# Two-layer hybrid attention encoder on one core: in the differential-attention steps, the next step's scores move ahead of the filler projection

## The chip, the core and the metric

The kernel runs on one core of a Trainium2 chip. The metric is device time of one execution in microseconds, as the median of several runs. A core has TensorE (PE: matmuls, with its weight loads shown as PEld), VectorE (DVE), ScalarE (ACT), GpSimd (POOL) and SyncE (SP, here only the queue of the weight transfers). Each engine works through its own list of instructions in the order in which the kernel wrote them, and a semaphore wait at the head of one list holds everything behind it in that list.

## What is computed

An encoder of two layers on 512 tokens of width 1024. Each layer: RMSNorm; one input projection; latent attention with 8 heads and differential attention with 4 heads; output projection with residual; RMSNorm; squared-ReLU MLP with residual. The part that the change touches is the differential attention, per head `hd` and block of 128 query rows:

```
dq, dk: (512, 4 heads, 2 maps, 64);  dv: (512, 4 heads, 128)
bias = -slope[hd] * |qpos - kpos|
s    = einsum('bqhmd,bkhmd->bmhqk', qb, k) * 64**-0.5 + bias     # two maps m per head
p    = softmax(s, axis=-1)
w    = p[:, 0] - lam * p[:, 1]
o    = einsum('bhqk,bkhd->bqhd', w, v);  o = rmsnorm(o) * g_sub * (1 - lam_init)
...
latent:  q = c_q @ w_uq (+rope),  [k, v] = c_kv @ w_ukv          # rank 256, 8 heads
```

All matmuls are done in split precision: each operand is a high and a low float32r part, and a product is three matmuls (high·high, high·low, low·high; helper `three`, line 1509).

## The kernel before

Everything stays in SBUF; weights stream in as blocks of 512 KB through two stage buffers, ScalarE makes the high part of a block (`split`, L748), VectorE or GpSimd the low part (L1064). The projections of the later work are cut into pieces and used as **filler** on TensorE between the pieces of attention.

The attention of a layer is one list of 48 steps, written out by hand for each engine: steps 0 to 15 are the differential attention (4 heads by 4 query blocks), steps 16 to 47 the latent attention. The table `FILL` (L68 to L96) says which filler belongs to a step: steps 0 to 7 carry half a head projection each (dk2, dk2, dq2, dq2, dk3, dk3, dq3, dq3; 12 matmuls of 128x512), steps 8 to 14 one latent product each (v0, v1, kp0, q0, v2, v3, q1; 6 matmuls of 128x512).

I name the pieces of step n on TensorE: **F**n the filler; **S**n+1 the score pair of the next step (`score_pair`, L1548: six matmuls on 64 rows, the two maps beside each other); **T**n-1 the four transposes of the weights w of the step before (`turn`, L1577); in every fourth step **V** the values of a head (`values`, 12 matmuls, L1509 with pt and dv; V0, V1, V2 in steps 6, 10, 14), and in other steps the sums (`stat_c`, L1523, steps 8 and 12) and the spread of the norm (`stat_b`, L1534, steps 9 and 13). Before the change a step is F, S, sum or spread or V, T.

A score pair has to wait for `sc_free`: there are three score banks for two maps, so S n+1 cannot start before VectorE has read the first map of pair n. That reading is `ttr` (L1094: adds the bias, takes the row maximum, writes e to SBUF). After it ScalarE does the exponential (L759), VectorE the coefficients (`coef`, L1105, L1106), GpSimd scales and subtracts (L625, L628, the result is w), TensorE transposes w (T), ScalarE and VectorE split it into pt_hi and pt_lo (L780, L1124), and four of those make V.

VectorE's list in step n is: coef n-1, `ttr` of both maps of pair n, pt_lo of n-3, the low part of the filler that ended two steps ago together with the low part of a weight block (L1064), then the filler that ended one step ago (L1134, L1138, or for v and kp L1163, L1170), then in steps 8 and 12 `rc` (L1363, waits for stat_c), in steps 9 and 13 the norm's product (L1369, waits for stat_b). In steps 6, 10 and 14 pt_lo stands first, ahead of coef. A filler needs its own bank (`bank0_free` or `bank1_free`, in turn) and its weight block; F10 (kp0) takes the bank of F8 (v0), which VectorE frees with L1163.

Of the kernel before, what the change touches and what calls it, by code (L numbers as in the profile page):

```python
# [50 lines left out]
DSTEPS = DIFF_HEADS * TT  # L51
# [163 lines left out]
def trunk(nc, x, w_in, g_mix, g_q, g_kv, w_uq, w_ukv, lam_q1, lam_k1, lam_q2, lam_k2,  # L215
# [89 lines left out]
    with ExitStack() as ctx:  # L305
# [68 lines left out]
        def val(sem, l, k):  # L374

            return (l + 1) * per_layer[id(sem)] + k
# [75 lines left out]
        def d_keys(g):  # L452

            if g == DIFF_HEADS - 1:
                return dk_last[:, 0, :], dk_last[:, 1, :]
            return dk_hi[:, g, :], dk_lo[:, g, :]
# [1047 lines left out]
        def _(pe):  # L1504
# [14 lines left out]
            def stat_c(l, m, src=None):  # L1519

                pe.wait_ge(misc_free, val(misc_free, l, m))
                for tt in range(TT):
                    mm = nc.tensor.matmul(MISC_BANK[:, tt:tt + 1], (ss[:, tt * P:(tt + 1) * P] if src is None  # L1523
                                                                   else src[:, tt * P:(tt + 1) * P]),
                                          ones[:, 0:1], start=True, stop=True)
                mm.then_inc(misc_done, 1)

            def stat_b(l, m, k):

                pe.wait_ge(pow_done, val(pow_done, l, k + 1))  # L1530
                pe.wait_ge(misc_free, val(misc_free, l, m))
                src = rs if k else rs_mix
                for tt in range(TT):
                    mm = nc.tensor.transpose(MISC_BANK[:, tt * P:(tt + 1) * P], src[:, tt:tt + 1].to_broadcast([P, P]), ident[:, :])  # L1534
                mm.then_inc(misc_done, 1)

            def score_pair(l, n):

                hd, qt = divmod(n, TT)
                if qt == 0:  # L1540
                    pe.wait_ge(d_lo_made, val(d_lo_made, l, 2 * hd + 2))
                pe.wait_ge(sc_free, val(sc_free, l, 2 * n - 1))
                q = slice(qt * P, (qt + 1) * P)
                k_hi, k_lo = d_keys(hd)
                for p, (a, b) in enumerate(((dq_hi, k_hi), (dq_hi, k_lo), (dq_lo, k_hi))):
                    for m in range(2):
                        rows = slice(m * DIFF_D, (m + 1) * DIFF_D)
                        mm = nc.tensor.matmul(SC_BANKS[(2 * n + m) % 3][:, :], a[rows, hd, q], b[rows, :],  # L1548
                                              start=p == 0, stop=p == 2)
                        if p == 2:  # L1550
                            mm.then_inc(sc_done, 1)

            def scores(l, n):

                hd, qt = divmod(n - DSTEPS, TT)
                e = DSTEPS + n
                if qt == 0:
                    pe.wait_ge(q_lo_made, val(q_lo_made, l, hd + 1))
                    pe.wait_ge(krb_lo_made, val(krb_lo_made, l, 1))
                    if hd:  # L1560
                        pe.wait_ge(krb_copied, val(krb_copied, l, 16 if hd < 2 else 48))
                    pe.wait_ge(*read_out(l, f"kp{hd // 2}"))
                pe.wait_ge(sc_free, val(sc_free, l, e - 2))
                three(SC_BANKS[e % 3][:, :],
                      [(tuple(q[:, qt * P:(qt + 1) * P] for q in q_tile(hd)),
                        (k_pack[:, hd % 4, 0, :], k_pack[:, hd % 4, 1, :]))], True, True).then_inc(sc_done, 1)
# [46 lines left out]
            def head_sum(l, use, part):  # L1613

                high, low = block_ready(l, BLOCK_AT[(use, 0)])
                pe.wait_ge(*high)
                pe.wait_ge(*low)
                pe.wait_ge(*taken(l, use))
                for t in part:
                    mm = three(bank[BANK[use]][:, :], [(wtile(SLOT[BLOCK_AT[(use, 0)]], t), u(t))], t == 0, t == KD - 1)  # L1620
                if part[-1] == KD - 1:
                    mm.then_inc(proj_done, 1)

            def out_sum(l, use, part):

                j, name = int(use[4:]), use[:4]
                high, low = block_ready(l, BLOCK_AT[(name, j // 2)])
                pe.wait_ge(*high)
                pe.wait_ge(*low)
                pe.wait_ge(*taken(l, use))  # L1630
                s = SLOT[BLOCK_AT[(name, j // 2)]]
                for t in part:
                    n = t if name == "outd" else DIFF_HEADS + t
                    pe.wait_ge(o_lo_made, val(o_lo_made, l, n + 1))
                    w = tuple(x[:, s, t * 256 + (j % 2) * P:t * 256 + (j % 2 + 1) * P] for x in (w_hi, w_lo))
                    mm = three(bank[BANK[use]][:, :], [(w, o_tile(n))], t == 0, t == TT - 1)
                if part[-1] == TT - 1:
                    mm.then_inc(proj_done, 1)

            def latent_sum(l, use):  # L1640

                pe.wait_ge(*taken(l, use))
                acc = bank[BANK[use]][:, :]
                i = int(use.lstrip("vqkp"))
                terms = []
                for k in range(KC):
                    block_at = BLOCK_AT[("uq" if use[0] == "q" else "ukv", k)]
                    s = SLOT[block_at]
                    high, low = block_ready(l, block_at)
                    pe.wait_ge(*high)  # L1650
                    pe.wait_ge(*low)
                    if use[0] == "q":
                        terms.append((wtile(s, i), (c_hi[:, k, :], c_lo[:, k, :])))
                        continue
                    wv = [t[:, s, :] for t in (w_hi, w_lo)]
                    if use[0] == "k":
                        terms.append((tuple(w[:, i * P:(i + 1) * P] for w in wv), (c_hi[:, KC + k, :], c_lo[:, KC + k, :])))
                    else:
                        terms.append((tuple(c[:, KC + k, i * P:(i + 1) * P] for c in (c_hi, c_lo)),
                                      tuple(w[:, MLA_HEADS * NOPE:] for w in wv)))  # L1660
                three(acc, terms, True, True).then_inc(proj_done, 1)
# [53 lines left out]
            for l in layers(pe):  # L1715
# [64 lines left out]
                for n in range(STEPS + 1):  # L1780
                    if DSTEPS < n + 2 < STEPS:
                        scores(l, n + 2)
                    g, r = divmod(n - TT - 2, TT)
                    for use, part in FILL.get(n, []):
                        if use[0] == "d":
                            head_sum(l, use, part)
                        elif use[0] == "o":
                            out_sum(l, use, part)
                        else:
                            if use == "v0":  # L1790
                                pe.wait_ge(c_lo_made, val(c_lo_made, l, 2 * KC))
                            latent_sum(l, use)
                    if n >= STEPS - 1:
                        out_sum(l, OUTM_USES[n - STEPS + 1], range(0, 2))
                    if n + 1 < DSTEPS:
                        score_pair(l, n + 1)
                    if r == 2 and 0 <= g < DIFF_HEADS:
                        stat_c(l, MISC_AT[f"sub{g}_c"], tmp_s[:, 1, :])
                    if r == 3 and 0 <= g < DIFF_HEADS:
                        stat_b(l, MISC_AT[f"sub{g}_b"], 3 + g)  # L1800
                    if r == 3 and g >= DIFF_HEADS:
                        half_values(l, g + 1, 0)
                    if r == 0 and g == DIFF_HEADS:
                        half_values(l, g, 0)
                    if r == 0 and g >= 0:
                        values(l, g)
                    if n:
                        turn(l, n - 1)
                    if n + 2 == DSTEPS:
                        scores(l, n + 2)  # L1810
# [190 lines left out]
```

## Time and profile before

| | |
|---|---|
| time before, median of 3 runs | 1214.62 us (1214.17 to 1215.73) |
| the profiled execution itself | 1214.01 us, of which the span from first to last instruction 1211.7 us |
| TensorE busy | 1190.8 us, 98% of the span |
| VectorE, ScalarE, GpSimd busy | 875.1, 600.8, 581.4 us |
| mean granted TensorE clock | 0.997 of full speed |
| differential attention, first layer | about 80 to 158 us of the span |
| differential attention, second layer | about 676 to 755 us of the span |

A profile row of the timeline gives the start of an instruction from the start of the span, its duration, the engine, the line of kernel.py, what it writes and reads, and in brackets the idle time of the engine before it with the instruction that ended it. Matmuls overlap in the record, so on TensorE the distance between two starts says what a piece costs, not the duration. The same holds for short operations on VectorE, which follow each other about 0.6 us apart where their own durations read 0.69.

### The profile page before, as it was taken

How to read it: one execution, taken by the hardware profiler on the slowest of the kernel's cores; microseconds unless marked ns; L12 is line 12 of the kernel's file. 1: busy time of each engine (PE TensorE's matmuls, PEld its weight loads, DVE VectorE, ACT ScalarE, POOL GpSimd, SP SyncE). 2: the span in 40 equal slices, each digit the busy share in tenths (PEclk: the TensorE clock that was granted, in tenths of full speed). 3: DMA queues.
4: the chain of work that ended last, by engine and by line, in shares of the span. 5: the costliest groups of instructions: out<-in, count | busy, mean ns of one | idle time of the engine just before them, and what ended most of it. 6: DMA issues, size and time to landing. Idle time of an engine off the chain costs nothing.

```text
span 1211.7 us, 16408 instructions
## 1 busy us (share of the span) xinstructions
PE 1190.8 (98%) x5700; PEld 974.7 (80%) x5700; DVE 875.1 (72%) x1349; ACT 600.8 (50%) x986; POOL 581.4 (48%) x371
## 2 busy tenths in 40 slices
PE   8999999999999999999999999999999999999997
PEld 7877678888888888888888766788888888888886
DVE  4657867656778776879846677776657778767896
ACT  6346666744544344435423466677444444344443
POOL 1004554622865576556510245536047665766462
PEclk9999999999999999999999999999999999999999
DMA  6421110124224322430324201102252234223402
GB/s 187 130 68 61 45 27 26 54 87 157 73 87 136 118 87 84 130 108 32 104 59 120 70 27 44 36 18 88 78 166 88 86 105 139 88 75 117 140 10 95
DMA packets 128131, 104.55 MB, mean 86 GB/s; under 512 B 5514, under 2 KB 107956, under 8 KB 128052
## 3 DMA queue, kind: packets, MB, share of 16 engines
q1 hardware_dynamic: 127840, 103.50, 28.5%
q8 instruction: 47, 0.77, 0.3%
q14 instruction: 32, 0.26, 0.1%
q10 hardware_dynamic: 84, 0.02, 0.0%
q0 software_dynamic: 128, 0.00, 0.0%
HBM read 99.84 MB, written 2.10 MB: 84 GB/s over the span
## 4 chain that ended last, share of the span: by engine, by line
PE 93%; DVE 3%; POOL 1%; issue 1%; ACT 1%; DMA 1%; SPq 0%; POOLq 0%; ACTq 0%; DVEq 0%
PE bank L1509 83%; PE bank L1577 3%; PE bank L1605 3%; PE bank L1548 2%; PE bank L1523 1%; DVE pt_lo L1124 1%; PE bank L1740 1%; DMA xin<-in_x 1%; PE bank L1534 0%; ACT pt_hi L780 0%; DVE k_pack L1170 0%; PE bank L1685 0%; POOL rs L619 0%; DVE dq_lo L1177 0%; POOL e_x L628 0%
## 5 line engine op out<-in xcount | busy, mean ns | idle before, releaser
L1509 PE MATMUL bank<-u_hi,w_hi 128*128 128x512 f32 x760 | 299.4, 394 | 0.3
L1509 PE MATMUL bank<-u_hi,w_lo 128*128 128x512 f32 x760 | 296.0, 390 | 0.0
L1509 PE MATMUL bank<-u_lo,w_hi 128*128 128x512 f32 x760 | 295.8, 389 | 0.0
L748 ACT ACTIVATE w_hi<-stage 128x1024 fp32r<-128x1024 f32 (+2 forms) x141 | 136.4, 976 | 221.1 <-DMA stage<-in_w_up 91.6
L1064 DVE TENSOR_TENSOR w_lo<-stage,w_hi 128x1024 fp32r<-128x1024 f32 (+2 forms) x116 | 137.4, 1193 | 60.4 <-ACT w_hi L748 60.0
L1509 PEld LDWEIGHTS bank<-u_hi,w_hi 128*128 128x128 f32 x760 | 142.7, 188 | 30.8 <-issue 2.5
L1509 PEld LDWEIGHTS bank<-u_hi,w_lo 128*128 128x128 f32 x760 | 142.6, 188 | 30.1
L1509 PEld LDWEIGHTS bank<-u_lo,w_hi 128*128 128x128 f32 x760 | 142.8, 188 | 28.6
L748 ACT ACTIVATE w_hi<-b 128x1024 fp32r<-128x1024 f32 x84 | 88.9, 1059 | 131.7 <-PE bank L1509 107.8
L1509 PE MATMUL bank<-w_hi,quad_hi 128*128 128x512 f32 x392 | 152.6, 389 | 0.0
L1509 PE MATMUL bank<-w_hi,quad_lo 128*128 128x512 f32 x392 | 152.5, 389 | 0.0
L1509 PE MATMUL bank<-w_lo,quad_hi 128*128 128x512 f32 x392 | 152.5, 389 | 0.0
L1064 DVE TENSOR_TENSOR w_lo<-b,w_hi 128x1024 fp32r<-128x1024 f32 x84 | 121.7, 1449 | 24.5 <-ACT w_hi L748 24.5
L1454 DVE TENSOR_TENSOR acc<-acc,bank 128x512 f32<-128x512 f32 x216 | 136.9, 680 | 0.0
L1124 DVE TENSOR_TENSOR pt_lo<-bank,pt_hi 128x512 fp32r<-128x512 f32 x96 | 66.1, 688 | 49.1 <-ACT pt_hi L780 48.7
L1468 DVE SCALAR_TENSOR_TENSOR tmp_y<-bank,rb 128x512 f32<-128x512 f32 x64 | 43.7, 689 | 69.2 <-PE bank L1509 68.5
L619 POOL TENSOR_TENSOR rs<-rc,mhalf 128x4 f32<-128x4 f32 x14 | 17.0, 1215 | 157.2 <-DVE rc L1079 143.2
L1509 PEld LDWEIGHTS bank<-w_lo,quad_hi 128*128 128x128 f32 x392 | 73.6, 188 | 15.4
L1509 PEld LDWEIGHTS bank<-w_hi,quad_lo 128*128 128x128 f32 x392 | 73.6, 188 | 15.2
L1509 PEld LDWEIGHTS bank<-w_hi,quad_hi 128*128 128x128 f32 x392 | 73.6, 188 | 15.2
L646 POOL TENSOR_TENSOR b<-b,b 128x1024 f32<-128x1024 f32 x28 | 81.6, 2913 | 2.0 <-DMA b<-in_w_down 1.0
L634 POOL TENSOR_SCALAR e_t<-e_t,coefs 128x512 f32<-128x512 f32 x64 | 44.2, 692 | 69.6 <-DVE coefs L1118 68.7
(236 smaller groups left out, 2287.0 us busy)
## 6 DMA issues: line engine op xcount, KB each, us to landing
stage<-in_w_up SPq DMA_DIRECT2D x64, 512.0 KB, 4.0
b<-in_w_down SPq DMA_DIRECT2D x56, 512.0 KB, 3.4
stage<-in_w_in SPq DMA_DIRECT2D x32, 512.0 KB, 3.9
stage<-in_w_out SPq DMA_DIRECT2D x16, 512.0 KB, 3.5
stage<-in_w_down SPq DMA_DIRECT2D x8, 512.0 KB, 3.4
xin<-in_x SPq DMA_DIRECT2D x4, 512.0 KB, 6.7
stage<-in_w_ukv SPq DMA_DIRECT2D x4, 512.0 KB, 3.8
out<-yout SPq DMA_DIRECT2D x8, 256.0 KB, 2.3
```

The lines of the kernel that those rows point to most:

```text
L619: nc.gpsimd.tensor_tensor(dst[:, :], rc[:, :], mhalf[:, :], ALU.pow).then_inc(pow_done, 1)
L634: nc.gpsimd.tensor_scalar(e_t[:, t, :], e_t[:, t, :], coefs[:, t:t + 1], 1.0, ALU.mult, ALU.mult).then_inc(p_ready, 1)
L646: nc.gpsimd.tensor_tensor(dst[:, :], a[:, :], b[:, :], ALU.subtract).then_inc(t_made, 1)
L748: last = nc.scalar.activation(hi(w_hi, s)[:, :, d:d + n], st(r)[:, :, f:f + n], ACT.Copy)
L1064: last = nc.vector.tensor_tensor(dst, st(r)[:, :, f:f + n], hi(w_hi, s)[:, :, d:d + n].bitcast(F32), ALU.subtract)
L1124: nc.vector.tensor_tensor(piece(pt_lo), TR_BANKS[n % 2].rearrange("p (k c) -> p k c", k=TT), piece(pt_hi).bitcast(F32), ALU.subtract).then ...
L1454: last = nc.vector.tensor_tensor(dst, dst, src, ALU.add)
L1468: nc.vector.scalar_tensor_tensor(out=tmp_y[:, i % 2, :], in0=bank[BANK[use]][:, :], scalar=0.0, in1=rb[:, :], op0=ALU.max, op1=ALU.mult).t ...
L1509: mm = nc.tensor.matmul(acc, a, b, start=first and t == 0 and m == 0, stop=last and t == len(terms) - 1 and m == 2)
L1548: mm = nc.tensor.matmul(SC_BANKS[(2 * n + m) % 3][:, :], a[rows, hd, q], b[rows, :], start=p == 0, stop=p == 2)
L1577: mm = nc.tensor.transpose(TR_BANKS[n % 2][:, kt * P:(kt + 1) * P], e_slot(t)[:, kt * P:(kt + 1) * P], ident[:, :])
L1605: mm = nc.tensor.matmul(MISC_BANK[:, q], v_pack[:, kt, hd, :, :].rearrange("p a c -> p (a c)"), pt[:, kt, q], start=(kt == 0 and pt is pt_ ...
```

## The change

In the step loop of TensorE the call of `score_pair(l, n + 1)` moves from behind the filler to ahead of it. Nothing else is edited: the number of instructions of every engine, their shapes, all semaphores and the orders of VectorE, ScalarE, GpSimd and SyncE are the same. It applies to the 15 steps 0 to 14 of each of the two layers, since a later step has no score pair.

```
@@ -1781,6 +1781,8 @@
                     if DSTEPS < n + 2 < STEPS:
                         scores(l, n + 2)
                     g, r = divmod(n - TT - 2, TT)
+                    if n + 1 < DSTEPS:
+                        score_pair(l, n + 1)
                     for use, part in FILL.get(n, []):
...
                         out_sum(l, OUTM_USES[n - STEPS + 1], range(0, 2))
-                    if n + 1 < DSTEPS:
-                        score_pair(l, n + 1)
```

TensorE, first layer, step 10, before: the last rows of T8, then F10 (reads c and w), S11 (reads dk and dq), and the first matmul of V1 (reads pt and dv). The semaphores that a matmul waits for stand in brackets.

```order
L1577 MATMUL bank<-ident,e_x 128x128 x3
L1509 MATMUL bank<-c_hi,w_hi 128x512 [waits w_hi_made,w_lo_dve,bank1_free]
L1509 MATMUL bank<-c_lo,w_hi 128x512
L1509 MATMUL bank<-c_hi,w_lo 128x512
...
L1548 MATMUL bank<-dk_hi,dq_hi 128x512 [waits sc_free]
L1548 MATMUL bank<-dk_hi,dq_hi 128x512
L1548 MATMUL bank<-dk_lo,dq_hi 128x512 x2
L1548 MATMUL bank<-dk_hi,dq_lo 128x512 x2
L1509 MATMUL bank<-pt_hi,dv_hi 128x512 [waits misc_free,pt_lo_made]
```

The same place with the change:

```order
L1577 MATMUL bank<-ident,e_x 128x128 x3
L1548 MATMUL bank<-dk_hi,dq_hi 128x512 [waits sc_free]
L1548 MATMUL bank<-dk_hi,dq_hi 128x512
L1548 MATMUL bank<-dk_lo,dq_hi 128x512 x2
L1548 MATMUL bank<-dk_hi,dq_lo 128x512 x2
L1509 MATMUL bank<-c_hi,w_hi 128x512 [waits w_hi_made,w_lo_dve,bank1_free]
L1509 MATMUL bank<-c_lo,w_hi 128x512
L1509 MATMUL bank<-c_hi,w_lo 128x512
...
L1509 MATMUL bank<-pt_hi,dv_hi 128x512 [waits misc_free,pt_lo_made]
```

The wait for `sc_free` now stands directly behind T8, and the six matmuls of the filler stand behind it, next to the values.

TensorE, first layer, step 9, before: the last rows of T7, then F9, S10, and the spread (`stat_b`).

```order
L1577 MATMUL bank<-ident,e_t 128x128 x3
L1509 MATMUL bank<-w_hi,c_hi 128x512 [waits w_hi_made,w_lo_dve,bank0_free]
L1509 MATMUL bank<-w_lo,c_hi 128x512
L1509 MATMUL bank<-w_hi,c_lo 128x512
...
L1548 MATMUL bank<-dk_hi,dq_hi 128x512 [waits sc_free]
L1548 MATMUL bank<-dk_hi,dq_hi 128x512
L1548 MATMUL bank<-dk_lo,dq_hi 128x512 x2
L1548 MATMUL bank<-dk_hi,dq_lo 128x512 x2
L1534 MATMUL bank<-ident,rs 128x128 [waits misc_free,pow_done]
```

The same place with the change:

```order
L1577 MATMUL bank<-ident,e_t 128x128 x3
L1548 MATMUL bank<-dk_hi,dq_hi 128x512 [waits sc_free]
L1548 MATMUL bank<-dk_hi,dq_hi 128x512
L1548 MATMUL bank<-dk_lo,dq_hi 128x512 x2
L1548 MATMUL bank<-dk_hi,dq_lo 128x512 x2
L1509 MATMUL bank<-w_hi,c_hi 128x512 [waits w_hi_made,w_lo_dve,bank0_free]
L1509 MATMUL bank<-w_lo,c_hi 128x512
L1509 MATMUL bank<-w_hi,c_lo 128x512
...
L1534 MATMUL bank<-ident,rs 128x128 [waits misc_free,pow_done]
```

Here too the filler has moved from ahead of the wait for `sc_free` to behind the score pair; the sum of the step before, T7 and the spread keep their places in the list.

## Rows read from the trace of the kernel before

**Rows 1.** Page, the chain that ended last: shares of the span by engine.

```profile
PE 93%; DVE 3%; POOL 1%; issue 1%; ACT 1%; DMA 1%; SPq 0%; POOLq 0%; ACTq 0%; DVEq 0%
```

**Rows 2.** Timeline, TensorE, step 4 (start, us, engine, line, what, count, idle before).

```profile
102.90 0.47 PE L1509 MATMUL bank<-u_hi,w_hi 128*128 128x512 f32 x1
...
105.84 0.50 PE L1548 MATMUL bank<-dk_hi,dq_hi 64*128 64x512 f32 x2
...
106.74 0.66 PE L1577 MATMUL bank<-ident,e_t 128*128 128x128 f32 x4
107.15 0.47 PE L1509 MATMUL bank<-u_hi,w_hi 128*128 128x512 f32 x1
```

**Rows 3.** Timeline, TensorE, steps 8 to 11 of the first layer.

```profile
124.21 0.50 PE L1548 MATMUL bank<-dk_hi,dq_hi 64*128 64x512 f32 x2
...
126.01 0.63 PE L1577 MATMUL bank<-ident,e_t 128*128 128x128 f32 x4
...
127.96 0.50 PE L1548 MATMUL bank<-dk_hi,dq_hi 64*128 64x512 f32 x2
...
130.20 0.66 PE L1577 MATMUL bank<-ident,e_x 128*128 128x128 f32 x4 [0.69 <-POOL e_x L628]
132.02 0.50 PE L1509 MATMUL bank<-c_hi,w_hi 128*128 128x512 f32 x1 [1.17 <-DVE v_pack L1163]
...
134.06 0.50 PE L1548 MATMUL bank<-dk_hi,dq_hi 64*128 64x512 f32 x2 [0.38 <-DVE nmx L1094]
...
137.82 0.60 PE L1577 MATMUL bank<-ident,e_t 128*128 128x128 f32 x4
```

**Rows 4.** Timeline, VectorE, steps 7 to 14 of the first layer.

```profile
120.16 1.35 DVE L1064 TENSOR_TENSOR w_lo<-stage,w_hi 128x768 fp32r<-128x768 f32 x3
...
126.53 0.67 DVE L1094 CUSTOM_DVE_ANT_0 e_t<-bank,consts 128x512 f32<-128x512 f32 x1
...
128.94 2.43 DVE L1064 TENSOR_TENSOR w_lo<-stage,w_hi 128x768 fp32r<-128x768 f32 x3
...
133.33 0.67 DVE L1094 CUSTOM_DVE_ANT_0 e_t<-bank,consts 128x512 f32<-128x512 f32 x1
...
141.60 0.69 DVE L1094 CUSTOM_DVE_ANT_0 e_t<-bank,consts 128x512 f32<-128x512 f32 x1
...
145.26 0.67 DVE L1094 CUSTOM_DVE_ANT_0 e_t<-bank,consts 128x512 f32<-128x512 f32 x1
...
148.79 0.74 DVE L1369 SCALAR_TENSOR_TENSOR tmp_s<-tmp_s,gsl,bank 128x512 f32<-128x512 f32 x1
...
150.24 0.67 DVE L1094 CUSTOM_DVE_ANT_0 e_x<-bank,consts 128x512 f32<-128x512 f32 x1
```

**Rows 5.** Timeline, GpSimd, the same stretch.

```profile
128.37 1.77 POOL L628 TENSOR_TENSOR e_x<-e_x 128x512 f32<-128x512 f32 x1
```

**Rows 6.** Timeline, TensorE, steps 12 to 16 of the first layer.

```profile
144.74 0.63 PE L1577 MATMUL bank<-ident,e_x 128*128 128x128 f32 x4
...
150.98 0.73 PE L1548 MATMUL bank<-dk_last,dq_hi 64*128 64x512 f32 x4 [0.19 <-DVE nmx L1094]
...
154.73 0.60 PE L1577 MATMUL bank<-ident,e_t 128*128 128x128 f32 x4
...
158.14 1.05 PE L1523 MATMUL bank<-ones,tmp_s 128*128 128x1 f32 x8 [0.29 <-ACT tmp_s L821]
```

**Rows 7.** Windows: stretch, length, busy of PE, PEld, DVE, ACT, POOL, then granted clock.

```profile
724.90:728.80 3.90, 2.05 (x13) 1.48 (x12) 3.90 (x7) 1.12 (x4) 1.27 (x1) 0.99 0.11 14
728.80:732.20 3.40, 3.40 (x11) 1.80 (x11) 2.93 (x11) 2.04 (x5) 2.25 (x3) 0.50 0.86 285
130.20:132.00 1.80, 0.65 (x4) 0.41 (x4) 1.80 (x5) 0.00 (x0) 0.00 (x0) 1.00 0.00 0
```

**Rows 8.** Timeline, TensorE, steps 10 and 11 of the second layer.

```profile
728.04 0.50 PE L1509 MATMUL bank<-c_hi,w_hi 128*128 128x512 f32 x1 [1.17 <-DVE v_pack L1163]
...
734.89 0.60 PE L1577 MATMUL bank<-ident,e_t 128*128 128x128 f32 x4
```

More of the change, by code:

```diff
@@ L1783, in _ @@
                     g, r = divmod(n - TT - 2, TT)
+                    if n + 1 < DSTEPS:
+                        score_pair(l, n + 1)
                     for use, part in FILL.get(n, []):
@@ L1794, in _ @@
                         out_sum(l, OUTM_USES[n - STEPS + 1], range(0, 2))
-                    if n + 1 < DSTEPS:
-                        score_pair(l, n + 1)
                     if r == 2 and 0 <= g < DIFF_HEADS:
```

## The prediction

> **What bounds the kernel now.** I read three views. The chain that ended last says that TensorE holds 93% of the span [rows 1]: whatever keeps TensorE idle counts in full. Then TensorE's timeline through the differential attention of the first layer. In steps 1 to 8 it never waits: step 4 costs 2.94 us for F, 0.90 for S and 0.41 for T [rows 2], and the other steps with twelve-matmul fillers repeat this. From step 9 on the fillers are only six matmuls and TensorE starts to wait: 0.69 us before T8 for w from GpSimd, 1.17 us before F10 for the bank that VectorE's v_pack frees, 0.38 us before S11 for the score bank [rows 3]. The third view, VectorE's own list, says why: between the score readings at 126.53 and 133.33 it works without a gap, 2.43 us of it on one weight block [rows 4]. So steps 9 to 14 are bound by VectorE's list, and TensorE has just enough other work in between. The second layer repeats the pattern 596 us later.
>
> **The sequence, written as a ring.** Before, TensorE does T(n-2), F(n), S(n+1), T(n-1); with the change T(n-2), S(n+1), F(n), T(n-1). Nothing is added or removed, no DMA moves, and no other engine's list changes. Three things change: which kinds of matmul are neighbours; T(n-1) gets one filler more between its scores and itself; and S(n+1) loses the filler that stood right before its wait for `sc_free`. Between S(n) and S(n+1) there stood T and F(n), now F(n-1) and T: equally much work, but one filler earlier against VectorE's list wherever VectorE is late.
>
> **Term 1, the neighbours: a small gain.** A filler after transposes and before scores costs 2.94 us [rows 2]; the twelve matmuls of V1, which stand between scores and transposes, cost 137.82 - 134.06 - 0.90 = 2.86 [rows 2, 3]. So the moved filler saves 0.08. Transposes directly followed by 64-row scores are in no row. Bounds: the transposes cost the same 0.41, or up to 0.1 more; the whole effect per step then lies between -0.08 and +0.02, and I take -0.05 to -0.06, since both neighbours of S already pay their turn today. Over the nine steps up to the sum of step 8 that is 0.5 us per layer: that sum ends at 125.5 instead of 126.01 [rows 3]. Limits: 0.8 earlier to 0.2 later.
>
> **Term 2, S10: nothing.** From here I replay the first layer against VectorE's list. VectorE starts the reading of pair 9 0.52 us after the sum of step 8 ends (126.53 against 126.01) [rows 3, 4], now at 126.0. A score pair starts 0.73 us after the reading that it waits for has begun (S11 134.06 against 133.33) [rows 3, 4]. So S10 starts at 126.75, where its place is free at 125.9: a new wait of 0.8 us. It costs nothing, because T8 waits for GpSimd's w, which hangs on that same sum: T8 comes at 130.2 - 0.5 = 129.7 (its releaser began at 128.37 and took 1.77 [rows 5]). S10, F9 (126.01 to 127.96 less 0.4 for T7, so 1.5) and the spread (0.4, four transposes like T) end at 126.75 + 0.9 + 1.5 + 0.4 = 129.55. The wait before T8 shrinks by what S10 waits for.
>
> **Term 3, S11: the main loss.** T8 ends at 130.1. S11 needs the reading of pair 10, which VectorE reaches at 133.33 - 0.5 = 132.8, so S11 starts at 133.55: TensorE stands still for 3.4 us. Before, F10 ran in part of this hole (132.02 to 134.06 with S11's wait). Now it comes after S11: S11 to 134.45, F10 (1.5) to 135.95, V1 (2.75 behind another matmul) to 138.7. Before it ended at 137.82 [rows 3]. So step 10 loses 0.9 us, although the step began 0.5 us early: the filler's 1.4 us are uncovered.
>
> **Term 4, S13: more of it.** VectorE and ScalarE wait for V1 before they can overwrite pt, so the reading of pair 12 follows the end of V1 by 141.60 - 137.82 = 3.8 us [rows 3, 4], now at 142.5. T9 and S12 and F11 and T10 run from 138.7 to 141.9 (0.4, 0.9, 1.5, 0.4), S13 has to stand until 142.5 + 0.73 = 143.2. Then S13 to 144.1, F12 to 145.6, the sum (124.21 to 126.01 less 0.9, so 0.9 [rows 3]) to 146.45. T11 stood at 144.74 [rows 6]: 1.7 us late.
>
> **Term 5, S14 and S15.** The reading of pair 13 follows that sum by 0.52 (145.26 against 144.74 [rows 4, 6]): S14 starts at 147.7 instead of following T11 at 146.9. S14, F13 and the spread end at 150.5. VectorE's product with the spread (148.79 before) is followed 1.45 us later by the reading of pair 14 (150.24) [rows 4]; with 150.6 for the product, S15 starts at 150.6 + 1.45 + 0.73 = 152.8 instead of 150.98 [rows 6]. S15, F14 and V2 end at 152.8 + 0.9 + 1.5 + 2.75 = 157.9. Before it was 154.73 [rows 6]. **Loss per layer: 3.2 us**, rounded to 3.1 for small parts that I rounded up.
>
> **Term 6, is it given back?** The next wait of TensorE, before the sum at 158.14, is for ScalarE's square of what stands behind V2 [rows 6]. It moves with V2, so the loss stays. From step 16 on the order is as it was. Two layers: +6.2 us. Limits per layer: 1.9 and 4. The lower one: VectorE's weight block of step 9 took 2.43 us, the same three instructions one block earlier 1.35 [rows 4]; if it fell to 1.35, S11 would come 1.1 us earlier. The row shows that the long one began inside GpSimd's 1.77 us [rows 4, 5] and ended about 1.2 us after it. Both follow the sum of step 8, so I keep 2.43. The Trainium skill's page "SBUF — State Buffer", section "Who interferes with whom", says that a VectorE operation with two SBUF inputs and a GpSimd operation that reads SBUF exclude each other for a whole instruction; by that rule the block stays at 2.43 as long as GpSimd begins first, and the trace agrees with it.
>
> **Term 7, TensorE's clock.** In the second layer, after a stretch in which TensorE had 2.05 us of work in 3.90, the granted clock fell to 0.50 for 3.4 us (728.8 to 732.2); in the same place of the first layer it stayed at 1.00 [rows 7]. That is 1.2 instead of 2.4 GHz. Its cost is read from F10 to T9: 6.85 us there (728.04 to 734.89), 5.80 in the first layer [rows 3, 8], so 1.05. With a hole of 3.4 us in the same place, and work without a pause behind it, I expect the low clock in both layers. Half speed for 3.4 us of full work costs 1.7, the row shows 1.05; I take 1.4. The first layer pays 1.4, the second 1.4 - 1.05 = 0.35, since it pays already. Sum 1.75 us; limits -1.05 (high clock in both) and +2.4. "TensorE: Matmul & The Clock Gate" of the Trainium skill, in "Part 1: The HAM clock gate", says that idling throttles the array to half rate and sustained work releases it; by that page the longer hole makes the low clock more likely, and one row here agrees while another, with a shorter hole, shows no drop.
>
> **The sum.** 6.2 + 1.75 = 8.0 us. The span of 1211.7 becomes 1219.7, the profiled execution of 1214.01 becomes 1222.0, and the median, 0.6 above it, 1222.6.
>
> **Rivals.** (a) *The waits come, the clock doesn't fall further.* If neither layer falls: 6.2 - 1.05 = +5.1, 1219.8; if one does, near 1221. For it: the first layer's hole left the clock at 1.00 [rows 7]. Against: the new hole is twice as long. (b) *VectorE is earlier than in my replay*, as by the 1.35 us block: 3.1 - 1.1 = 2.0 per layer, +4.0 and little from the clock, 1218.6. Against: the lists of VectorE and GpSimd keep their order. (c) *No change that can be told.* The early scores let VectorE pull its readings forward everywhere, and S11 finds its bank free soon enough that F10 loses only what T8 and F10 wait for now: the 0.7 and 1.2 us [rows 3] pay for it, 1214.6. Against: between 126.53 and 133.33 VectorE has no gap to pull anything into [rows 4]. (d) *Faster.* T has one filler more before it. If the waits before T8 (0.69) and F10 (1.17) [rows 3] really went and nothing came in their place, each layer would win 1.9 less what the next step returns, about 1.2, with 0.5 of Term 1 on top: -3.4 us, 1211.2. It decides at one point: VectorE would have to start the reading of pair 10 by 129.4, so that S11 follows T8 at 130.1; it starts at 132.8. (e) *Worse*: the low clock comes a second time at the holes before S13 and S15, 1.4 in each layer, 1225.4.
>
> **How the numbers follow.** Forecast (both layers with the low clock) 45%; (a) 23%; (b) 12%; (c) 8%; (d) 6%; (e) 6%. The range leaves out (c) and (d) and the far end of (e): 1217.0 to 1225.5, which holds about 82%; its lower end is (b) with a limit of Term 1, its upper end the forecast with 1.7 per low clock, a loss of 4 in one layer, and (e). A measurement of this kernel can tell about 0.2%, 2.4 us: slower by more takes the forecast, (a), (e) and most of (b), 0.84; within 0.2% takes (c) and a little of (b), 0.10; faster 0.06.
>
> **What would show it.** In the changed profile: steps 1 to 8 of a layer at about 4.2 us without a wait; a wait before S10 of under 1 us; a wait of some 3.4 us before S11, released by VectorE's L1094, in place of the waits before F10; S13 and S15 with waits of 1 to 2 us; V2 of the first layer ending near 157.9; a granted clock of 0.5 behind S11 in both layers. I am wrong if S11 starts within 1 us of T8's end, if V2 ends before 155.5, or if the delay is gone again by step 20.

## The result and the profile after

| | before | changed |
|---|---|---|
| median | 1214.39 us, 4 runs (1213.85 to 1215.73) | 1229.01 us, 4 runs (1224.91 to 1229.34) |
| profiled execution | 1214.01 us | 1229.19 us |
| its span | 1211.7 us | 1226.8 us |
| mean granted clock | 0.997 | 0.991 |

The changed kernel is slower: ratio 1.0106, 95% interval 1.0094 to 1.0118, which is 12.9 us (11.4 to 14.3). The two medians are 14.6 us apart and the spans of the two profiled executions, which are taken apart below, 15.1 us. The forecast was slower by 8.0 us (1222.6), with a range up to 1225.5. The direction holds, the size doesn't.

The page of the changed kernel: the span, then the busy time of each engine. TensorE is busy for 98% of the span, the same share as before. But its busy time rose from 1190.8 to 1197.9 us with the same 5700 matmuls: at a low clock a matmul is busy for longer. This is the first hint that about half of the loss isn't waiting.

```profile
span 1226.8 us, 16408 instructions
...
PE 1197.9 (98%) x5700; PEld 982.8 (80%) x5700; DVE 877.9 (72%) x1349; ACT 602.0 (49%) x986; POOL 581.5 (47%) x371
```

**Steps 1 to 8.** Timeline of TensorE of the changed kernel, step 4 (columns as in [rows 2]). F, then T, then the scores directly behind T, then the next F:

```profile
103.54 0.50 PE L1509 MATMUL bank<-u_hi,w_hi 128*128 128x512 f32 x1
...
106.44 0.60 PE L1577 MATMUL bank<-ident,e_t 128*128 128x128 f32 x4
106.97 0.50 PE L1548 MATMUL bank<-dk_hi,dq_hi 64*128 64x512 f32 x2
...
107.86 0.50 PE L1509 MATMUL bank<-u_hi,w_hi 128*128 128x512 f32 x1
```

F took 106.44 - 103.54 = 2.90 where it was 2.94 [rows 2]. S took 0.89 as before. T took 106.97 - 106.44 = 0.53 where it was 0.41. The step grew from 4.25 to 4.32 us. No step up to 7 has a wait.

**Steps 8 to 15.** The same view, first layer, to be laid beside [rows 3] and [rows 6]. Scores are L1548, transposes L1577, the sum behind V2 L1523:

```profile
125.78 0.63 PE L1577 MATMUL bank<-ident,e_t 128*128 128x128 f32 x4
127.03 0.50 PE L1548 MATMUL bank<-dk_hi,dq_hi 64*128 64x512 f32 x2 [0.62 <-DVE nmx L1094]
...
129.99 0.66 PE L1577 MATMUL bank<-ident,e_x 128*128 128x128 f32 x4
133.85 0.80 PE L1548 MATMUL bank<-dk_hi,dq_hi 64*128 64x512 f32 x2 [3.21 <-DVE nmx L1094]
...
141.70 0.60 PE L1577 MATMUL bank<-ident,e_t 128*128 128x128 f32 x4
...
146.24 0.74 PE L1548 MATMUL bank<-dk_last,dq_hi 64*128 64x512 f32 x4 [0.99 <-DVE nmx L1094]
...
150.69 0.73 PE L1548 MATMUL bank<-dk_last,dq_hi 64*128 64x512 f32 x4 [0.61 <-DVE nmx L1094]
...
155.90 0.73 PE L1548 MATMUL bank<-dk_last,dq_hi 64*128 64x512 f32 x4 [1.79 <-DVE nmx L1094]
...
162.63 0.60 PE L1577 MATMUL bank<-ident,e_t 128*128 128x128 f32 x4
...
166.04 1.05 PE L1523 MATMUL bank<-ones,tmp_s 128*128 128x1 f32 x8 [0.28 <-ACT tmp_s L821]
```

The waits before T8 (0.69) and F10 (1.17) of [rows 3] are gone. In their place S10 waits 0.62, S11 3.21, S13 0.99, S14 0.61 and S15 1.79, each for VectorE's reading of an earlier score pair: 7.2 us in all.

VectorE's own timeline of the changed kernel shows that it is no earlier than before. These are the reading of pair 9, the weight block and the reading of pair 10, the ones of [rows 4]:

```profile
126.30 0.67 DVE L1094 CUSTOM_DVE_ANT_0 e_t<-bank,consts 128x512 f32<-128x512 f32 x1
...
128.70 2.45 DVE L1064 TENSOR_TENSOR w_lo<-stage,w_hi 128x768 fp32r<-128x768 f32 x3
...
133.12 0.67 DVE L1094 CUSTOM_DVE_ANT_0 e_t<-bank,consts 128x512 f32<-128x512 f32 x1
```

The reading of pair 10 moved from 133.33 to 133.12 and no further. VectorE's timeline shows no gap from 126.30 to there.

**The clock.** Windows of the changed kernel (columns as in [rows 7]; behind the clock come the share of DMA and its GB/s). The first three follow the hole before S11; then come the low stretch behind S15, the one behind S11 in the second layer, and one that comes later in that layer:

```profile
130.70:133.00 2.30, 0.00 (x0) 0.00 (x0) 2.30 (x7) 0.00 (x0) 0.00 (x0) 1.00 0.28 55
133.00:133.90 0.90, 0.05 (x2) 0.05 (x2) 0.90 (x6) 0.07 (x1) 0.59 (x1) 0.52 1.08 375
133.90:139.70 5.80, 5.80 (x16) 4.18 (x17) 2.60 (x9) 1.97 (x5) 3.50 (x4) 0.50 0.29 101
157.00:160.50 3.50, 3.50 (x9) 2.76 (x9) 1.55 (x7) 0.92 (x3) 2.54 (x3) 0.52 0.00 0
737.30:744.10 6.80, 5.73 (x16) 4.11 (x17) 3.72 (x14) 2.04 (x5) 4.10 (x4) 0.51 0.43 145
771.00:774.50 3.50, 3.50 (x13) 2.72 (x11) 0.78 (x2) 1.27 (x3) 2.53 (x3) 0.55 0.01 2
```

TensorE did nothing from 130.7 to 133.0. At about 133.0 the granted clock fell to 0.5, that is 1.2 instead of 2.4 GHz, while TensorE was still idle. It stayed there until 139.7, through 5.8 us of work without a pause. It came once more from 157.0 to 160.5. In the second layer it lasted again 6.8 us behind S11 and 3.5 us after the attention steps. This execution has 20.5 us of it. The kernel before had the 3.4 us of [rows 7] and as much again near the start of its profiled execution, where the changed kernel had none. The same window of both, before and then changed:

```profile
8.50:12.00 3.50, 3.50 (x14) 2.59 (x13) 2.58 (x5) 2.38 (x5) 0.00 (x0) 0.51 1.14 323
8.50:12.00 3.50, 3.50 (x20) 2.89 (x19) 3.04 (x5) 3.05 (x6) 0.00 (x0) 1.00 1.15 324
```

Both kernels have the same instructions in the same order there, so this isn't the change's doing. But the same matmuls, from the first of L1685 to the first of L1705, took 6.40 us before (10.07 to 16.47) and 5.55 in the changed kernel (10.29 to 15.84). This is why the changed kernel's first layer begins early: its first score pair stands at 79.38 instead of 80.02, and 0.63 of these 0.64 us are there at 16 us already.

**The price of the low clock** is read from pieces with the same instructions. S11 to T9 takes 141.70 - 133.85 = 7.85 us. In a run below whose clock stayed up (the one with idle matmuls) it takes 139.12 - 134.00 = 5.12: 2.73 us lost. S15 to T13 takes 162.63 - 155.90 = 6.73 against 158.54 - 153.43 = 5.11 in that run: 1.62 lost. The second layer:

```profile
738.37 0.79 PE L1548 MATMUL bank<-dk_hi,dq_hi 64*128 64x512 f32 x2 [3.21 <-DVE nmx L1094]
...
746.04 0.60 PE L1577 MATMUL bank<-ident,e_t 128*128 128x128 f32 x4
...
760.24 0.73 PE L1548 MATMUL bank<-dk_last,dq_hi 64*128 64x512 f32 x4 [1.79 <-DVE nmx L1094]
...
765.36 0.60 PE L1577 MATMUL bank<-ident,e_t 128*128 128x128 f32 x4
...
770.69 0.66 PE L1577 MATMUL bank<-ident,e_t 128*128 128x128 f32 x4 [0.86 <-POOL e_t L628]
```

Here S11 to T9 takes 7.67 (2.55 lost) and S15 to T13 5.12 (nothing lost). From the 770.69 on to the last values takes 6.18, in the kernel before 4.60: 1.58 lost. In all 8.5 us, where the kernel before loses 1.05 in the second layer and the 0.64 of its start.

### The profile page after: what moved, and what is told of

The parts are those of the page before. It is cut to its first block, busy times and chain, and to the rows that moved or that the text cites. A ratio compares the mean times of both kernels' runs of the same rounds, so it can differ in the third digit from the quotient of the medians.

```text
span 1226.8 us, 16408 instructions
## 1 busy us (share of the span) xinstructions
PE 1197.9 (98%) x5700; PEld 982.8 (80%) x5700; DVE 877.9 (72%) x1349; ACT 602.0 (49%) x986; POOL 581.5 (47%) x371
## 4 chain that ended last, share of the span: by engine, by line
PE 94%; DVE 3%; issue 1%; ACT 1%; POOL 1%; DMA 0%; POOLq 0%; SPq 0%; ACTq 0%; DVEq 0%
PE bank L1509 83%; PE bank L1577 3%; PE bank L1605 2%; PE bank L1548 2%; PE bank L1523 1%; DVE pt_lo L1124 1%; PE bank L1534 1%; PE bank L1740 1%; PE bank L1677 0%; DMA xin<-in_x 0%; ACT pt_hi L780 0%; DVE k_pack L1170 0%; PE bank L1685 0%; DVE dq_lo L1177 0%; PE bank L1893 0%
## 5 line engine op out<-in xcount | busy, mean ns | idle before, releaser
L1064 DVE TENSOR_TENSOR w_lo<-stage,w_hi 128x1024 fp32r<-128x1024 f32 (+2 forms) x116 | 137.0, 1190 | 60.6 <-ACT w_hi L748 60.1
L1454 DVE TENSOR_TENSOR acc<-acc,bank 128x512 f32<-128x512 f32 x216 | 137.0, 680 | 0.0
L780 ACT ACTIVATE pt_hi<-bank 128x512 fp32r<-128x512 f32 x96 | 57.1, 594 | 49.7 <-PE bank L1509 30.8
```

The source lines that it names most:

```text
L780: nc.scalar.activation(pt_hi[:, :, q * P:(q + 1) * P], TR_BANKS[n % 2].rearrange("p (k c) -> p k c", k=TT), ACT.Copy).then_inc(pt_hi_made, 1)
L1064: last = nc.vector.tensor_tensor(dst, st(r)[:, :, f:f + n], hi(w_hi, s)[:, :, d:d + n].bitcast(F32), ALU.subtract)
L1454: last = nc.vector.tensor_tensor(dst, dst, src, ALU.add)
```

## The experiments

Each ran in five rounds beside the kernel before. They were measured in three groups. The kernel before had medians of 1215.26, 1215.76 and 1215.90 us in these, and a ratio is always against the runs of the same group.

**Which steps carry the loss.** The move was made in some steps only. In all of these the edit has one form; the condition is all that differs:

```diff
-                    if n + 1 < DSTEPS:
+                    if n + 1 < DSTEPS and <condition>:
                         score_pair(l, n + 1)
                     for use, part in FILL.get(n, []):
...
+                    if n + 1 < DSTEPS and not (<condition>):
+                        score_pair(l, n + 1)
                     if r == 2 and 0 <= g < DIFF_HEADS:
```

Only the steps with long fillers, condition `n < 8`:

> The score pair is moved ahead of the filler only in steps 0 to 7 (twelve-matmul fillers), steps 8 to 14 stand as before. My theory: in these steps TensorE has no holes, so only the junction of transposes and scores costs, 0.06 us in each of some six steps per layer: 1214.4 + 0.8 = 1215.2 us, no wait in steps 1 to 8, clock as before. Rival (the whole delay comes from the long fillers now ending late against VectorE and ScalarE): most of the 14.6 us is here, 1222 us or more.

Measured 1215.71 us, ratio 1.0001 (0.9993 to 1.0010). The long fillers cost nothing that can be told. TensorE's timeline of this run still shows what the new neighbours cost: T8 stands at 130.20, as in [rows 3], although the layer's first score pair, which stands in the same place in every kernel, began at 79.58 instead of 80.02 us; 0.44 us went on the way. It also shows the low clock in a place where the kernel before had none in its profiled execution. This is S11 with 0.80 instead of 0.50 per pair of matmuls, and T9 at 138.88 instead of 137.82 [rows 3]:

```profile
130.20 0.66 PE L1577 MATMUL bank<-ident,e_x 128*128 128x128 f32 x4 [0.69 <-POOL e_x L628]
...
134.19 0.80 PE L1548 MATMUL bank<-dk_hi,dq_hi 64*128 64x512 f32 x2
...
138.88 0.60 PE L1577 MATMUL bank<-ident,e_t 128*128 128x128 f32 x4
```

So the order before brings the low clock from time to time too, and the 1.05 us of Term 7 are read here a second time.

Only the steps from 8 on, condition `n >= 8`:

> The score pair is moved only in steps 8 to 14. My theory: the holes before S11, S13 and S15 and the low clock behind them come back in full, 14.6 less 0.8 = +13.8, 1228.2 us. Rival (long fillers): under +4, 1218 us at most.

Measured 1228.2 us (1226.63 to 1229.74), ratio 1.0107 (1.0093 to 1.0121), the same as the whole change. The loss lies where TensorE waits for VectorE. The hole before S11 was 3.21 us here too. In the first layer of this execution S11 to T9 took 6.65 us, 1.5 more than at the full clock, where the changed kernel lost 2.7; in the second it took 7.92, 2.8 more.

Only step 10, condition `n == 10`:

> The score pair is moved in step 10 alone. My theory: S11 starts when VectorE has read pair 10, as before at about 134 us, and F10 comes behind it: V1 is 1.5 us later per layer, and the hole of about 3.4 us before S11 brings the low clock, 2.7 us in the first layer and 1.6 more in the second: 3.0 + 4.3 = +7.3, 1221.7 us; without the low clock +3, 1217.4. Rival (it is the sum of small shifts in all of steps 8 to 14, each of which takes from the next): about a seventh of the whole, +2, 1216.5 us.

Measured 1221.5 us, ratio 1.0051 (1.0037 to 1.0065), +6.2. TensorE's timeline of this run, the transposes of step 8 and the scores S11 behind them, then T9:

```profile
130.07 0.66 PE L1577 MATMUL bank<-ident,e_x 128*128 128x128 f32 x4 [0.69 <-POOL e_x L628]
133.94 0.80 PE L1548 MATMUL bank<-dk_hi,dq_hi 64*128 64x512 f32 x2 [3.21 <-DVE nmx L1094]
...
141.89 0.60 PE L1577 MATMUL bank<-ident,e_t 128*128 128x128 f32 x4
```

One moved score pair in each layer gives the full hole of 3.21 us. Up to T8 nothing differs from [rows 3], where it stands at 130.20 with the same wait of 0.69. T9 comes at 141.89 instead of 137.82: 1.4 us for the filler that no longer runs in the hole, and 2.8 for the clock (S11 to T9 takes 7.95 instead of 5.12), less the 0.1 by which S11 came earlier. The hole doesn't come from the steps ahead.

Only step 9, condition `n == 9`:

> The score pair is moved in step 9 alone. My prediction says that this is free: S10 waits 0.8 us, but T8 waits for GpSimd's w in any case, and nothing else is late: within 0.5 us of before, T8 at the same time. Rival (every early wait costs what it lasts): +0.8 per layer, +1.6 us.

Measured 1216.0 us, ratio 1.0002 (0.9994 to 1.0011). S10 waits for VectorE in this run too (0.61 us), and this costs nothing: T7 to T8 takes 4.21 us (127.86 to 132.07), before it took 4.19 [rows 3]. The wait of 0.69 before T8 is gone, so S10 now waits in the time in which T8 used to wait for GpSimd. F10's wait for v_pack is still 1.16, as in [rows 3].

Only steps 12 and 14, condition `n in (12, 14)`:

> The score pair is moved in steps 12 and 14 alone. My theory (the loss sits where a filler is taken from in front of a wait that VectorE ends): S13 starts 0.73 us after the reading of pair 12 begins (141.6), at 142.3, and F12 behind it ends 0.9 us later than S13 did; S15 starts at 151.0 as before, with F14 (1.4 us) behind it: 2.3 us per layer, 4.6 in all, and the hole of 1.8 us before S15 brings a low clock of 1.6 us in about one of the layers: 1215.3 + 4.6 + 1.6 = 1221.5 us, 1219.9 without it. Rival (step 10 is the one place, and the later waits only follow from it): no wait before S13 and S15 of over 0.5 us, 1216 us.

Measured 1221.7 us (1220.12 to 1221.9), ratio 1.0051 (1.0038 to 1.0063), +5.8. The scores S13 and S15 and the T13 behind V2:

```profile
142.16 0.73 PE L1548 MATMUL bank<-dk_last,dq_hi 64*128 64x512 f32 x4 [1.06 <-DVE nmx L1094]
...
151.60 0.74 PE L1548 MATMUL bank<-dk_last,dq_hi 64*128 64x512 f32 x4 [1.57 <-DVE nmx L1094]
...
156.73 0.60 PE L1577 MATMUL bank<-ident,e_t 128*128 128x128 f32 x4
```

S13 waits 1.06 and S15 1.57, though nothing was moved in step 10, and T13 comes 2.0 us later than the 154.73 of [rows 6] at a full clock. This layer began 0.27 us earlier (first score pair at 79.75), so it lost 2.3, as was expected. Of the 5.8 us some 4.5 are this, and the low clock, which this execution shows twice in the second layer, can account for the rest.

All steps but 10, 12 and 14, condition `n not in (10, 12, 14)`:

> The score pair is moved in all of the steps 0 to 14 but 10, 12 and 14. My theory: the waits that appear before S10 and S14 are covered by the waits for GpSimd before T8 and T12, and only the junction of transposes and scores is left, about 0.06 us in each of some nine steps per layer: 1215.3 + 1 = 1216.3 us. Rival (the move costs something wherever it stands): eleven fifteenths of the 14.6 us less the low clock, +5 or more, 1220 us.

Measured 1217.27 us, ratio 1.0007 (0.9998 to 1.0016), +1.4. That isn't clear of noise. Its runs fall into two sets: five from 1214.3 to 1215.8 us with a mean clock of 0.998, six from 1217.3 to 1218.0 with 0.995. The profiled one is of the second set and had the low clock from 8.1 to 15.0 us, ahead of everything that was moved. The three parts sum to 6.2 + 5.8 + 1.4 = 13.4 us, where the whole cost 14.6 in its own runs and 12.9 as steps 8 on. The rival that the loss is spread over all steps, and Term 1's gain, both fall; three steps carry some nine tenths of it.

**Is it the clock?** In the changed kernel the holes were filled with idle matmuls. Twelve stand ahead of S11, four ahead of S13, seven ahead of S15. They write into the first of the two banks that the scores are about to fill, once that is free:

```diff
-                pe.wait_ge(sc_free, val(sc_free, l, 2 * n - 1))
+                pe.wait_ge(sc_free, val(sc_free, l, 2 * n - 2))
...
+                for _ in range({11: 12, 13: 4, 15: 7}.get(n, 0)):
+                    nc.tensor.matmul(SC_BANKS[2 * n % 3][:, :], dq_hi[:, hd, q], k_hi, start=True, stop=True)
+                pe.wait_ge(sc_free, val(sc_free, l, 2 * n - 1))
```

> The changed kernel with idle-filling matmuls (128x512 on operands already in SBUF, into the bank that S writes next) in the holes: 12 before S11, 4 before S13, 7 before S15, each behind the wait for that bank and ahead of the wait for VectorE. They add 23 matmuls per layer and no result. My theory (the low clock is a cost of its own beside the waits): the granted clock stays at 1.00 and the kernel gains 2.7 + 1.6 in the first layer and 2.6 + 1.6 in the second, 8.5 together: 1220.5 us, V2 of the first layer ends 4 us earlier. Rival (the waits are the cost, the low clock only fills time that TensorE would wait in anyway): within 1 us of the changed kernel, 1229 us; it could also be slower, if the extra matmuls push the scores later.

Measured 1222.79 us (1221.94 to 1225.14), ratio 1.0064 (1.0052 to 1.0076): 6.2 us less than the changed kernel, with 46 matmuls more, whose products are not used. TensorE's timeline and the windows (scores are L1551 here, transposes L1580, the idle matmuls L1546):

```profile
130.55 3.01 PE L1546 MATMUL bank<-dk_hi,dq_hi 128*128 128x512 f32 x12
134.00 0.50 PE L1551 MATMUL bank<-dk_hi,dq_hi 64*128 64x512 f32 x2 [0.44 <-DVE nmx L1094]
...
139.12 0.60 PE L1580 MATMUL bank<-ident,e_t 128*128 128x128 f32 x4
...
153.43 0.74 PE L1551 MATMUL bank<-dk_last,dq_hi 64*128 64x512 f32 x4 [0.19 <-DVE nmx L1094]
...
158.54 0.60 PE L1580 MATMUL bank<-ident,e_t 128*128 128x128 f32 x4
```

```profile
130.50:134.00 3.50, 3.06 (x15) 2.20 (x13) 3.50 (x11) 0.02 (x1) 0.55 (x1) 1.00 0.41 126
134.00:140.00 6.00, 6.00 (x32) 4.60 (x34) 2.65 (x9) 2.65 (x7) 3.58 (x4) 1.00 0.29 102
764.00:767.40 3.40, 3.28 (x10) 2.77 (x11) 1.21 (x3) 1.58 (x4) 2.96 (x4) 0.54 0.01 2
```

S11 starts at 134.00, 0.15 later than in the changed kernel, still released by VectorE. T8 was 0.15 later already (130.14), so the idle matmuls put nothing on top: T8 to S11 takes 3.86 us in both. But T9 comes at 139.12 instead of 141.70 and T13 at 158.54 instead of 162.63. The clock stood at 1.00 through the hole and after it. One low stretch remained in this execution, after the differential attention of the second layer. The forecast of 8.5 us less had none in it. It costs 1.6 us, as in the changed kernel, and that is what separates this execution (1222.15) from the expected 1220.5; the median lies 0.6 above it. So the rest of the loss is there without the clock: this span of 1220.3 less 1.6 is 1218.7, and the span before, 1211.7 less its own 1.05 and 0.64, is 1210.0. That leaves 8.7 us, and some 7 of the 15.1 for the clock.

The same cure for the kernel before, five idle matmuls in the gap between T8 and F10:

```diff
+                    if n == 10:
+                        pe.wait_ge(sc_free, val(sc_free, l, 2 * n))
+                        for _ in range(5):
+                            nc.tensor.matmul(SC_BANKS[2 * (n + 1) % 3][:, :], dq_hi[:, n // TT, 0:P], d_keys(n // TT)[0], start=True, stop=True)
                     for use, part in FILL.get(n, []):
```

> The kernel before with five matmuls that give no result (128x512, into the bank of S11) between T8 and F10, where TensorE stands idle for 1.4 us. My theory (low clock as a cost of its own): the second layer's low clock at 728 to 732 us, 1.05 us, does not come: -1, 1213.9 us. Rival (the hole is not what brings it): no change, and 0.5 granted clock in the same place.

Measured 1215.65 us, ratio 0.9996 (0.9987 to 1.0005): a miss. The windows say why:

```profile
130.00:133.00 3.00, 2.99 (x13) 1.84 (x11) 3.00 (x9) 0.00 (x0) 0.14 (x1) 1.00 0.37 101
160.00:163.50 3.50, 3.50 (x10) 2.63 (x9) 0.47 (x1) 1.18 (x3) 2.24 (x3) 0.51 0.00 0
```

The place that was filled kept its clock, in both layers. But the low clock came elsewhere in that execution, at 160.0 and again at 757.3, each behind a wait of 0.86 us for GpSimd. Filling one gap of a chain with several doesn't buy the 1 us.

**Is it VectorE's list?** The weight block of step 9 stands on VectorE ahead of the reading of pair 10. It was moved behind the reading of pair 11, to the end of step 10. Its user comes much later. This was done on the kernel before and on the changed one:

```diff
-                    split(l, BLOCK_AT[(use, 0)] + RING)
+                    if use != HEAD_USES[-1]:
+                        split(l, BLOCK_AT[(use, 0)] + RING)
...
                         elif use[0] not in "vk":
                             gen(l, use)
+                    if n == 10:
+                        split(l, BLOCK_AT[(HEAD_USES[-1], 0)] + RING)
```

> The kernel before, with one edit on VectorE: the low part of the last query-weight block (L1064, 2.43 us in step 9) is made at the end of step 10 instead, behind the readings of pair 10 and v1. My theory (VectorE's list in steps 9 and 10 sets when TensorE goes on): v_pack frees F10's bank at about 129.5 instead of 131.9 and the reading of pair 10 begins at 131.0 instead of 133.3; F10 follows T8 at once, V1 ends at 135.4 instead of 137.8: 2.4 us per layer and the second layer's low clock (1) go: -5.8, 1209 us. Rival (the waits before F10 and S11 are only shown there, the chain through GpSimd and ScalarE sets the pace): within 1 us of before.

Measured **1209.11 us** (1207.95 to 1210.89), ratio 0.9946 (0.9934 to 0.9958), the fastest kernel of this case. TensorE's timeline, the starts of F10 (L1512 here), S11 and T9:

```profile
130.33 0.48 PE L1512 MATMUL bank<-c_hi,w_hi 128*128 128x512 f32 x1
...
131.90 0.50 PE L1551 MATMUL bank<-dk_hi,dq_hi 64*128 64x512 f32 x2
...
135.66 0.60 PE L1580 MATMUL bank<-ident,e_t 128*128 128x128 f32 x4
```

VectorE's, the reading of pair 10 and the moved block:

```profile
130.72 0.67 DVE L1094 CUSTOM_DVE_ANT_0 e_t<-bank,consts 128x512 f32<-128x512 f32 x1
...
132.53 1.74 DVE L1064 TENSOR_TENSOR w_lo<-stage,w_hi 128x768 fp32r<-128x768 f32 x3
```

The reading starts at 130.72 instead of 133.33 [rows 4]. F10 and S11 follow each other and T8 without a wait, and T9 comes at 135.66 instead of 137.82 [rows 3]. T8 (129.92) was 0.28 earlier already, so a layer gains 1.9 us and not the 2.4 that I expected. The rest goes with the clock: its mean was 0.999, and the profiled execution has no low stretch at all before its idle end.

> The changed kernel with the same edit. My theory: the reading of pair 10 begins at about 131.4, S11 starts at 132.1 instead of 133.9, the hole before it falls from 3.4 to 1.7 us and leaves the clock high: 1.7 us of waiting and 2.6 us of low clock less per layer: 1229 - 8.6 = 1220.4 us; it stays slower than the same edit on the kernel before, by about 11 us, since S13 and S15 still wait ahead of their fillers. Rival (the changed order is bad whatever VectorE does): gain as small as on the kernel before, 5 us at most, 1224 us.

Measured 1222.45 us (1218.6 to 1224.57), ratio 1.0052 (1.0039 to 1.0065), 6.6 less than the changed kernel but 2 more than expected. TensorE's timeline, S11 and T9:

```profile
132.43 0.50 PE L1551 MATMUL bank<-dk_hi,dq_hi 64*128 64x512 f32 x2 [1.59 <-DVE nmx L1094]
...
139.15 0.60 PE L1580 MATMUL bank<-ident,e_t 128*128 128x128 f32 x4
```

and a window of the same run:

```profile
132.00:137.00 5.00, 4.57 (x15) 3.41 (x16) 4.65 (x14) 2.05 (x5) 3.31 (x4) 0.66 0.10 17
```

The hole before S11 shrank from 3.2 to 1.6 us and T9 came 2.5 us earlier. But in this layer the clock fell all the same, for half as long (133.6 to 137.0); in the second, behind a hole of 1.6 us too, it stayed up. Two more low stretches came at 164.3 and at 754. Even with VectorE unloaded the changed order is 13 us behind the old one: S13 and S15 still wait 1.0 and 1.8 us.

## Why the prediction was right about the sign and short by half

**Term 1, the neighbours: wrong in sign.** I bounded the transposes in front of 64-row scores at up to 0.1 more and took a gain for the step. They cost 0.12 more (0.53 against 0.41), F gave back 0.04 and not 0.08, and the step grew by 0.07. From the layer's first score pair (79.38, before 80.02) to T8 (129.99, before 130.20) the changed kernel takes 0.43 us more, in the second layer 0.39, where 0.5 less was forecast. Two layers: 1.8 us of the miss.

**Term 2, S10: right.** Forecast: S10 at 126.75 with a wait of 0.8, free of charge, T8 at 129.7. Measured: 127.03, 0.62, 129.99. The run with step 9 alone shows the wait and no loss.

**Term 3, S11: right.** Forecast: a hole of 3.4 us, S11 at 133.55, by L1094. Measured: 3.21 and 133.85. The run with step 10 alone shows that this one move makes the hole. V1 was to end at 138.7; with the clock held up it ended at 139.12, with the low clock at 141.70.

**Terms 4 and 5, S13 to S15: right but for the clock.** S13, S14, S15 and the end of V2 were forecast at 143.2, 147.7, 152.8 and 157.9. Take the 2.73 us of clock behind S11 from the measured times, and for the end of V2 the 1.62 of the second low stretch too: 143.5, 148.0, 153.2 and 158.3. All are 0.3 to 0.4 late: the 0.9 of Term 1 less the 0.64 by which this execution's first layer began early. That they lie so close is in part luck, since those two cancel. The run with idle matmuls has the end of V2 at 158.54. The 3.1 us per layer stand but for the 0.9 of Term 1.

**Term 6, not given back: right.** T13 comes 7.9 us later than in [rows 6], and so does the sum, 166.04 against 158.14. The second layer begins 7.9 us late and the span ends 15.1 late.

**The limits of Term 6.** The weight block took 2.45 us again, so rival (b) fell. GpSimd's instruction (L628) took 1.79 beside it. With the block moved away that instruction still took 1.78, so its length doesn't come from the block. What stands ahead of it in all three runs is VectorE's dq_lo (L1158, two SBUF inputs), which begins 0.03 us before it; in most other steps L628 takes 1.3 us. The block, for its part, ends 1.2 us after GpSimd's instruction in all three: 131.37 after 130.14 before, 131.15 after 129.93 changed, and 134.27 after 133.06 with the block moved, where it meets the next step's L628:

```profile
131.77 1.29 POOL L628 TENSOR_TENSOR e_t<-e_t 128x512 f32<-128x512 f32 x1
```

It takes 2.43, 2.45 and 1.74 us there, and 1.35 where no L628 runs (120.16 [rows 4]). So each of the two engines is held up once by the other, in the order in which they began. This agrees with the rule from "SBUF — State Buffer" of the Trainium skill, section "Who interferes with whom", that the two exclude each other for a whole instruction.

**Term 7, the clock: the term that was mis-sized.** Forecast 1.75 us: 1.4 for one low stretch in the first layer and 0.35 more in the second. Measured 8.5 - 1.05 = 7.4 us, or 6.8 if the 0.64 at the start of the kernel before is counted too. Two things failed. I took the price of a stretch from [rows 7, 8], where the low clock ended after 3.4 us. Behind the hole of 3.2 us it lasted for 6.7 to 6.8 in this execution, and cost 2.7 and 2.55. And I gave a second stretch per layer 6% (rival (e)), priced at 1.4 each; it came in both layers and cost 1.6 each, though in the second layer not at the holes that I named but after them, where the order is the old one. The run with the idle matmuls in the kernel before and the one with step 9 alone have a low stretch at that place of the first layer too (160.0 and 161.9 us), so that one may not be the change's doing. "TensorE: Matmul & The Clock Gate" of the Trainium skill says in "Part 1: The HAM clock gate" that idling throttles the array to half rate. The hole before S11 agrees in both layers, and the run that fills it confirms it. My last sentence under Term 7 misread its rows: the layer whose clock stayed up has the same two waits (0.69 before T8, 1.17 before F10) as the one whose clock fell, not shorter ones. For the shorter holes the runs give no rule (below).

**The balance.** From the layer's first score pair to T13 the first layer took 8.5 us more than before (7.9 and the 0.64 of its early start) and the second 5.65. Take out the clock, 4.35 in the first and 2.55 - 1.05 = 1.5 in the second: 4.2 and 4.15 are left, where 3.1 were forecast. 0.9 of the 1.1 between them is Term 1, 0.5 not gained and 0.4 paid. So the span's 15.1 is 8.3 of waits and neighbours (forecast 6.2) and 6.8 of clock (forecast 1.75), the 0.64 at the start counted as clock of the kernel before. The clock makes up 5 of the 7 us by which the forecast fell short, Term 1 nearly all of the rest. Rival (d) needed VectorE to start the reading of pair 10 by 129.4, and (c) needed it pulled forward; it started at 133.12.

## What to carry to other kernels

Before an engine's work is put in another order, look for what stands right before each wait in the old order: here it ran in a hole which VectorE makes anyway, and moving it behind the wait cost 1.4 us in step 10, its full time, and 2.3 us in steps 12 and 14 together. It cost nothing in step 9, where another wait behind it took up the delay. A hole in TensorE's work of some 3 us must be priced with the clock behind it, here 1.5 to 2.8 us on 5.1 us of work, and not with the hole alone. And where one engine's full list is what makes the others wait, the gain lies in that list: taking one weight block out of VectorE's way was worth 6.6 us, 3.8 of it in the waits of the two layers, and none of the orders tried on TensorE was worth anything.

## What the runs showed of the hardware that I had not expected

- The granted clock fell at all six holes of 3.2 us in the three profiled executions that have them (changed, steps from 8 on, step 10 alone): at the earliest 1.8 us before the hole ended (734.0, S11 at 735.77), at the latest 0.3 after (134.7, S11 at 134.41). S11 to T9 then took 6.65 to 7.95 us instead of 5.12.
- Apart from the idle end of the kernel, every low stretch of the twelve profiled executions lasted either 3.4 to 3.5 us or 6.7 to 6.9 us, though most of that was work without a pause. At the holes of 3.2 us it was the long kind five times of six.
- With holes of 1 to 2 us it comes and goes. The changed kernel had it behind the 1.79 us before S15 in the first layer and not in the second. With steps 12 and 14 alone, waits of 1.06 and 1.57 us left the first layer at full clock, and in the second layer it came twice. The kernel before had it behind a gap of 1.2 us in the second layer, the run with the long fillers moved had it in both. What decides there stays open; the spread of single runs (1224.91 to 1229.34) is of the size of one long and one short stretch.
- Twelve idle matmuls in the hole cost nothing that can be seen and saved 2.7 us behind it (7.85 against 5.12). They would be the cheap cure for a hole that can't be closed.
- Four transposes between a filler and 64-row scores cost 0.53 us, between scores and a filler 0.41; a filler followed by transposes instead of scores gave back only 0.04 of it.
